# Differential attention: where the ratio of the two softmaxes' sums is formed

## Chip, cores and metric

The kernel runs on 1 core of one Trainium2 chip. The metric is the device time of one execution in microseconds; less is better. It was measured as 2989.36 us, median of 3 runs (2987.06 to 2989.91).

## The reference

The program is two transformer blocks over 1024 tokens of width 1024, float32. The change touches one stage of the second block, differential attention, 4 heads with queries and keys of 64 and values of 128:

```python
s1 = einsum(q1, k1) * scale
s2 = einsum(q2, k2) * scale
p = softmax(s1) - lam * softmax(s2)
out = einsum(p, v)
```

`lam` is one scalar. With e1, e2 the exponentials and t1, t2 their row sums, the kernel uses p = (e1 - lam * t1/t2 * e2) / t1: it forms the ratio t1/t2 times -lam, combines the two unnormalised rows with it, and multiplies the result of the values by 1/t1 at the end.

## The kernel before

The five engines each run a program of stages in order, and semaphores order them against each other. Class `DiffAttention` is the stage in question. It handles M = 32 tiles m of 128 queries (4 heads, 8 tiles each); a tile's scores against all 1024 keys fill two PSUM banks for each of the two softmaxes, c = 0 and c = 1 (banks 0 to 3). In an iteration m of the engines' loops, with no bank spare for the scores:

- **TensorE** (`tensor`): turns the combined weights of tile m-2 in eight transposes (`turn`, L1583, banks 4 and 5), multiplies half of a pair's weights with the values in twelve matmuls (`attend`, L1596), then forms the scores of tile m+1: four matmuls of 512 columns for c = 0 and four for c = 1 (`scores`, L1573). Each of the two groups waits until ScalarE's exponential of tile m has read its banks. Every other iteration it turns two results back (`back`, L1607).
- **ScalarE** (`scalar`): in even iterations it takes a result out (`take`, L1662); it copies the high parts of the turned weights of tile m-2 out of PSUM (`high`, two of 512 columns, L1656); in `exps` it shifts the peak to a bias of one element a partition (L1631) and takes the exponential of c = 0 (L1643, out to tile `both`, with an accumulator read that gives the row sum), then that of c = 1 (L1643 too, out to tile `diff`); in odd iterations it scales two results (`finish`, L1672).
- **VectorE** (`vector`): two peaks of tile m (`peak`, L1696), two low parts of tile m-2 (`low`, L1718), then for tile m-1 `weigh`: the reciprocal of both sums (L1703) and the ratio (L1707, one element a partition), and the `combine` (L1713) over 1024 columns.
- **GpSimd** parts the next head's queries, keys and values into high and low (L1497 to L1532), stores a head's result, and near the end parts the first operands of the next attention (L1225, L1227). SyncE loads them.

So VectorE's order in an iteration is peak, peak, low, low, reciprocal, ratio, combine, and ScalarE's is (take), high, high, bias, exponential, exponential, (finish). The combine of tile m-1 follows the ratio, and TensorE's turn of it follows the combine, one iteration later. A peak of tile m waits for its score group, and the exponential c = 0 for the bias, the exponential c = 1 for the second peak.

Of the kernel before, what the change touches and what calls it, by code (L numbers as in the profile page):

```python
# [25 lines left out]
ACT = mybir.ActivationFunctionType  # L26
ALU = mybir.AluOpType
# [14 lines left out]
class Core:  # L42


    def __init__(self, nc, ctx, words, parts_words):

        self.nc, self.ctx = nc, ctx
        self.parts_words = parts_words
        self.arena = ctx.enter_context(nc.sbuf_tensor("arena", [P, words], F32))
        self.arena_at = nc.sbuf_base - 4 * words  # L50
        self.psum = ctx.enter_context(nc.psum_tensor("psum", [P, 8, HALF], F32))
        self.words, self.top = words, 0
        self.plain, self.parts_ctx = False, None
        self.open_parts("parts_mixer")
        self.free, self.used, self.total_cleared, self.arrivals = [], [], 0, 0
        self.pool_stored = [ctx.enter_context(nc.semaphore(f"pool_stored{s}")) for s in range(2)]
        self.pool_stored_count = [0, 0]
# [69 lines left out]
class Stage:  # L127
# [8 lines left out]
    def scalar(self, act):  # L136
        pass

    def vector(self, dve):
        pass  # L140
# [5 lines left out]
class Part(Stage):  # L146


    def __init__(self, done=(), sync=None, tensor=None, scalar=None, vector=None, gpsimd=None):
        self.done, self.methods = list(done), (sync, tensor, scalar, vector, gpsimd)  # L150
# [47 lines left out]
def hold(engine, conditions):  # L198

    for sem, value in conditions:  # L200
        engine.wait_ge(sem, value)
# [871 lines left out]
class WideAttention:  # L1073
# [286 lines left out]
    def turned_half(self, h):  # L1360
        return self.core.psum[:, 4 + h, :].rearrange("p (b t) -> p b t", t=P)
# [68 lines left out]
class DiffAttention:  # L1430
# [5 lines left out]
    def __init__(self, core, name, q, k, v, out, neg_lam, neg_shift, loads_after, first_free, rest_free, pe_after, act_after, own, sets, shared):  # L1436


        self.core, self.q, self.k, self.v, self.out = core, q, k, v, out
        self.neg_lam, self.neg_shift = neg_lam, neg_shift  # L1440
        self.loads_after, self.first_free, self.rest_free = loads_after, first_free, rest_free
        self.pe_after, self.act_after, self.ahead = pe_after, act_after, []
        self.M = self.HEADS * TT
        self.pT, self.p0 = shared
        here = [own.take(3, S, dtype=F32R) for c in range(2)]
        self.qk = [[sets[0], here[1]], [here[0], sets[1]]]
        self.vp = [sets[2], own.take(2, TT, P, dtype=F32R)]
        self.p1 = own.take(2, S)
        self.qs, self.ks, self.vs = own.take(2, S), own.take(2, S), own.take(TT, self.DV)
        self.os_, self.oT = own.take(2, TT, self.DV), own.take(2 * P)  # L1450
        self.nmax, self.bias, self.ratio = own.take(4), own.take(2), own.take(2)
        self.total, self.inv = own.take(8, 2), own.take(8, 2)
        s = core.sem
        self.loaded, self.v_loaded = core.sems(f"{name}_loaded", 2), s(f"{name}_v_loaded")
        self.parted, self.v_parted = core.sems(f"{name}_parted", 2), s(f"{name}_v_parted")
        self.scored, self.peaked, self.neg_ready, self.shifted, self.expd = (
            s(f"{name}_{x}") for x in ("scored", "peaked", "neg_ready", "shifted", "expd"))
        self.inverted, self.ratio_ready, self.combined = s(f"{name}_inverted"), s(f"{name}_ratio_ready"), core.sems(f"{name}_combined", 2)
        self.opened = s(f"{name}_opened")
        self.turned, self.high_out, self.low_out = s(f"{name}_turned"), s(f"{name}_high_out"), s(f"{name}_low_out")  # L1460
        self.attended, self.taken, self.backed, self.finished = (
            s(f"{name}_{x}") for x in ("attended", "taken", "backed", "finished"))
        self.stored, self.stored_before = core.pool_stored, list(core.pool_stored_count)
        for c in range(2):
            core.pool_stored_count[c] += 16 * self.HEADS // 2
        self.stage_free = core.sems(f"{name}_stage_free", 2)
        self.done = [(self.stage_free[c], self.HEADS // 2) for c in range(2)]
        self.exps_done = [(self.expd, 2 * self.M)]
        self.results_out = [(self.finished, self.M // 2)]
        self.even_set_free = [(self.scored, 6 * TT), (self.attended, 3 * TT // 2)]  # L1470
# [156 lines left out]
    def exps(self, act, m, c):  # L1627
# [14 lines left out]
        src = self.core.psum[:, 2 * c:2 * c + 2, :].rearrange("p a b -> p (a b)")  # L1642
        act.activation(dst, src, ACT.Exp, bias=bias, accum_out=self.total[:, m % 8, c:c + 1]).then_inc(self.expd, 1)  # L1643

    def turned_half(self, h):
        return self.core.psum[:, 4 + h, :].rearrange("p (b t) -> p b t", t=P)

# [27 lines left out]
    def scalar(self, act):  # L1675
        M = self.M
        hold(act, self.act_after)
        for m in range(M + self.LAG):
            if m % 2 == 0 and 0 <= m - 6 < M:
                self.take(act, (m - 6) // 2)  # L1680
            if 0 <= m - 2 < M:
                self.high(act, m - 2)
            if m < M:
                self.exps(act, m, 0)
                self.exps(act, m, 1)
            if m % 2 and 0 <= m - 7 < M:
                self.finish(act, (m - 7) // 2)
# [7 lines left out]
        spot = self.nmax[:, at:at + 1]  # L1695
        dve.tensor_reduce(spot, src, AX.X, ALU.max, negate=True).then_inc(self.neg_ready if c else self.peaked, 1)  # L1696

    def weigh(self, dve, m):

        dve.wait_ge(self.expd, 2 * m + 2)  # L1700
        if m >= 8:
            dve.wait_ge(self.finished, m // 2 - 3)
        dve.reciprocal(self.inv[:, m % 8], self.total[:, m % 8]).then_inc(self.inverted, 1)  # L1703
        dve.wait_ge(self.inverted, m + 1)
        if m >= 2:
            self.wait_combined(dve, m - 2)
        dve.tensor_scalar(self.ratio[:, m % 2:m % 2 + 1], self.total[:, m % 8, 0:1], self.inv[:, m % 8, 1:2], self.neg_lam,  # L1707
                          ALU.mult, ALU.mult).then_inc(self.ratio_ready, 1)

    def combine(self, engine, m):  # L1710

# [9 lines left out]
    def vector(self, dve):  # L1721
        M = self.M
        hold(dve, self.act_after)
        for m in range(M + self.LAG):
            if m < M:
                self.peak(dve, m, 0)
                self.peak(dve, m, 1)
            for h in range(2):
                if 0 <= m - 2 < M:
                    self.low(dve, m - 2, h)  # L1730
            if 0 <= m - 1 < M:
                self.weigh(dve, m - 1)
                if (m - 1) % TT not in self.BY_POOL:
                    self.combine(dve, m - 1)

# [3185 lines left out]
```

## Time and profile before

| | us |
|---|---|
| median of 3 runs | 2989.36 |
| the profiled execution's own time | 2981.91 |
| its span | 2980.2 |
| PE busy | 2830.7 (95%) |
| DVE busy | 1765.6 (59%) |
| POOL busy | 1345.3 (45%) |
| ACT busy | 1174.8 (39%) |
| the stage touched, first to last scores | 2448.1 to 2622.4 |

PE is TensorE's matmuls and PEld its weight loads, DVE VectorE, ACT ScalarE, POOL GpSimd. The shares are over the whole program; the stage touched is about 190 us of it, between the projections of the second layer and the latent attention. PEclk is the granted TensorE clock as a share of full speed. A row of a timeline gives start, duration, engine, line, operation, what it writes and reads, shapes and the number of instructions merged; brackets hold the idle time before and what ended it. Since engines overlap the end of one instruction with the start of the next, the cost of an instruction in a row of them is best read from start to start.

### The profile page before, as it was taken

The numbers are of one execution on the slowest core, as the hardware profiler recorded it, in microseconds if no ns is written. First come the engines' busy times: TensorE is split into PE (matmuls) and PEld (weight loads), VectorE is DVE, ScalarE is ACT, GpSimd is POOL, SyncE is SP. The second block draws the span as 40 slices with busy tenths as digits, with TensorE's granted clock in tenths as the row PEclk, the third lists the DMA queues.
The fourth block names the chain that finished last, engine by engine and source line by source line (L and its number), as shares of the span: only waits on it lengthen the run. The fifth ranks groups of instructions, "written<-read, shape, count | busy, mean of one in ns | idle before, by whom it ended". The sixth has DMA issues, their size and how long they took to land.

```text
span 2980.2 us, 42866 instructions
## 1 busy us (share of the span) xinstructions
PE 2830.7 (95%) x15248; PEld 2379.3 (80%) x15248; DVE 1765.6 (59%) x3125; ACT 1174.8 (39%) x2142; POOL 1345.3 (45%) x962
## 2 busy tenths in 40 slices
PE   7999998899999999999999999999999978889999
PEld 6688957777888878888888788987888776678877
DVE  3799937448666651313057578971224849978861
ACT  3311167243222221313123457761323536767750
POOL 2233124555777776663255334335341534333235
PEclk9999998899999999999999999999999999999999
DMA  3123243332222125443865442405426753131223
GB/s 138 65 96 134 68 115 75 125 113 81 85 85 85 45 88 203 125 141 123 150 203 181 127 113 67 117 22 174 151 84 227 223 152 75 46 79 36 84 85 128
DMA packets 224371, 336.30 MB, mean 113 GB/s; under 512 B 81911, under 2 KB 152439, under 8 KB 223687
## 3 DMA queue, kind: packets, MB, share of 16 engines
q1 hardware_dynamic: 200790, 289.88, 32.4%
q10 hardware_dynamic: 22192, 39.98, 3.7%
q0 software_dynamic: 1216, 4.20, 0.5%
q8 instruction: 102, 1.67, 0.2%
q14 instruction: 71, 0.57, 0.1%
HBM read 235.20 MB, written 98.81 MB: 112 GB/s over the span
## 4 chain that ended last, share of the span: by engine, by line
PE 85%; DVE 5%; issue 3%; ACT 2%; DMA 2%; POOL 1%; SPq 1%; DVEq 0%; POOLq 0%; ACTq 0%; PEldq 0%
PE psum L737 16%; PE psum L2924 15%; PE psum L2568 8%; PE psum L3259 8%; PE psum L444 7%; PE psum L1275 4%; PE psum L1306 4%; PE psum L1286 4%; PE psum L530 3%; PE psum L1573 2%; PE psum L984 2%; PE psum L962 1%; PE psum L973 1%; PE psum L2033 1%; PE psum L2243 1%
## 5 line engine op out<-in xcount | busy, mean ns | idle before, releaser
L2924 PE MATMUL psum<-parts_ffn 128*128 128x512 f32 x1200 | 285.5, 393 | 3.7 <-issue 2.0
L737 PE MATMUL psum<-parts_even,parts_ffn 128*128 128x512 f32 (+1 forms) x1344 | 288.1, 376 | 0.0
L737 PE MATMUL psum<-parts_odd 128*128 128x496 f32 (+1 forms) x1344 | 269.9, 361 | 6.2 <-POOL parts_odd L652 5.3
L737 PEld LDWEIGHTS psum<-parts_even,parts_ffn 128*128 128x128 f32 x1344 | 239.1, 189 | 44.6
L2924 PEld LDWEIGHTS psum<-parts_ffn 128*128 128x128 f32 x1200 | 227.0, 189 | 53.6 <-issue 2.2
L737 PEld LDWEIGHTS psum<-parts_odd 128*128 128x128 f32 x1344 | 227.2, 191 | 41.9 <-POOL parts_odd L652 5.5
L444 PE MATMUL psum<-parts_mixer 128*128 128x512 f32 x912 | 210.0, 391 | 0.3 <-DVE parts_mixer L287 0.3
L444 PEld LDWEIGHTS psum<-parts_mixer 128*128 128x128 f32 x912 | 170.4, 188 | 35.8 <-DVE parts_mixer L287 0.5
L2311 DVE TENSOR_SCALAR_CACHE_REDUCE choose_flags<-arena,choose_bits 128x384 uint8<-128x384 f32 (+2 forms) x198 | 174.3, 943 | 1.2
L3259 PE MATMUL psum<-parts_ffn 128*128 128x512 f32 x720 | 167.3, 389 | 2.9 <-DVE arena L3065 1.6
L2924 PE MATMUL psum<-up_t,parts_ffn 128*128 128x512 f32 x684 | 168.7, 394 | 0.0
L3259 PEld LDWEIGHTS psum<-parts_ffn 128*128 128x128 f32 x720 | 135.0, 188 | 31.9 <-DVE arena L3065 2.1
L773 ACT ACTIVATE arena<-psum 128x512 f32<-128x512 f32 (+4 forms) x120 | 60.6, 520 | 240.7 <-PE psum L737 238.8
L2924 PEld LDWEIGHTS psum<-up_t,parts_ffn 128*128 128x128 f32 x684 | 128.0, 187 | 30.8
L3847 DVE SCALAR_TENSOR_TENSOR arena<-arena 128x64 f32<-128x64 f32 (+1 forms) x464 | 133.9, 369 | 0.6
L402 POOL CAST parts_mixer<-arena 128x1024 fp32r<-128x1024 f32 (+1 forms) x23 | 29.0, 1261 | 225.8 <-PE psum L444 109.1
L2999 ACT ACTIVATE arena<-psum,arena 128x1024 f32<-128x1024 f32 x44 | 53.0, 1207 | 189.9 <-DVE psum L3094 158.9
L3065 DVE SCALAR_TENSOR_TENSOR arena<-psum,arena 128x1023 f32<-128x1023 f32 x88 | 111.0, 1280 | 26.0 <-ACT arena L2999 24.4
L3236 POOL TENSOR_TENSOR parts_ffn<-arena,parts_ffn 128x1024 fp32r<-128x1024 f32 x44 | 118.4, 2691 | 3.5
L2558 POOL TENSOR_TENSOR out_ring<-arena,out_ring 128x1024 fp32r<-128x1024 f32 x48 | 115.7, 2411 | 3.8
L2556 POOL CAST out_ring<-arena 128x1024 fp32r<-128x1024 f32 x48 | 51.6, 1075 | 137.3 <-PE psum L2568 118.8
L1275 PE MATMUL psum<-latent 96*128 96x512 f32 x384 | 101.8, 401 | 1.6 <-ACT both L1341 1.2
(419 smaller groups left out, 6466.4 us busy)
## 6 DMA issues: line engine op xcount, KB each, us to landing
arena<-ffn_down_k SPq DMA_DIRECT2D x44, 512.0 KB, 3.7
arena<-x SPq DMA_DIRECT2D x8, 2048.0 KB, 9.6
x<-arena SPq DMA_DIRECT2D x24, 512.0 KB, 3.9
arena<-w_in_e SPq DMA_DIRECT2D x24, 512.0 KB, 4.6
e_tokens<-arena ACTq DMA_DIRECT2D x24, 512.0 KB, 3.3
arena<-w_in_o SPq DMA_DIRECT2D x24, 496.0 KB, 6.1
arena<-ffn_up_b SPq DMA_DIRECT2D x11, 1024.0 KB, 4.9
up_raw_two<-ffn_up_b SPq DMA_DIRECT2D x11, 1024.0 KB, 4.9
```

The costliest lines, as they stand in the source:

```text
L444: last = pe.matmul(self.bank(s, h), self.weights.parts[:, s, a, k, :], self.hT[:, b, k, h * HALF:(h + 1) * HALF], start=(k, a, b) == (0, 0 ...
L737: last = pe.matmul(self.bank(t, n), self.hT[:, a, k, t * P:(t + 1) * P], w, start=(k, a, b) == (0, 0, 0), stop=(k, a) == (KT - 1, 1))
L1275: last = pe.matmul(ps[:, 2 * (n % 2) + b, :], queries, keys[:, b * HALF:(b + 1) * HALF], start=m == 0, stop=m == len(pairs) - 1)
L1286: last = pe.transpose(ps[:, 4 + h, j * P:(j + 1) * P], self.p[:, n % 2, b * P:(b + 1) * P], self.core.ident)
L1306: last = pe.matmul(ps[:, 6, 0:2 * P], values, self.pT[:, g % 2, part, b], start=(b, m) == (0, 0), stop=(b, m) == (KT - 1, len(pairs) - 1))
L2311: last = dve.tensor_scalar(self.flags[j], w, self.bits[:, j:j + 1].bitcast(F32), None, op, ALU.add, accum_out=self.count[:, j:j + 1])
L2558: pool.tensor_tensor(low, self.raw[:, n % 2], high.bitcast(F32), ALU.subtract).then_inc(self.w_low, 1)
L2568: last = pe.matmul(self.core.psum[:, 2 * t + h, :], self.catT[:, b, k, (4 * g + t) * P:(4 * g + t + 1) * P], w[:, c, h * HALF:(h + 1) * HA ...
L2924: last = pe.matmul(self.core.psum[:, bank, :], slot[:, a, k, :], operand[b][:, k, :], start=opens and (k, a, b) == (0, 0, 0), stop=(k, a) ...
L3236: pool.tensor_tensor(low, self.raw[:, n % 2], high.bitcast(F32), ALU.subtract).then_inc(self.w_low, 1)
L3259: last = pe.matmul(self.core.psum[:, 2 * t + h, :], a[:, b, t * P:(t + 1) * P], w[:, c, h * HALF:(h + 1) * HALF], start=(k, m) == (0, 0), ...
L3847: last = dve.scalar_tensor_tensor(out=x, in0=x, scalar=self.ss[:, n % 2, head + h:head + h + 1], in1=gain, op0=ALU.mult, op1=ALU.mult)
```

## The change

ScalarE, not VectorE, forms the ratio. In iteration m it does so for tile m-1 between its two exponentials, in two one-element copies: the sum t1 times the reciprocal of t2, and, after a wait for that, the result times -lam. `weigh` on ScalarE waits for VectorE's reciprocal and, for its two-deep buffer, for the combine of tile m-3. VectorE keeps the reciprocal, now in `invert`, and does it ahead of the low parts instead of behind them; the combine stays behind the low parts.

```diff
@@ -1448,13 +1448,14 @@
         self.p1 = own.take(2, S)
         self.qs, self.ks, self.vs = own.take(2, S), own.take(2, S), own.take(TT, self.DV)
         self.os_, self.oT = own.take(2, TT, self.DV), own.take(2 * P)
-        self.nmax, self.bias, self.ratio = own.take(4), own.take(2), own.take(2)
+        self.nmax, self.bias, self.ratio, self.share = own.take(4), own.take(2), own.take(2), own.take(2)
         self.total, self.inv = own.take(8, 2), own.take(8, 2)
         s = core.sem
         self.loaded, self.v_loaded = core.sems(f"{name}_loaded", 2), s(f"{name}_v_loaded")
         self.parted, self.v_parted = core.sems(f"{name}_parted", 2), s(f"{name}_v_parted")
         self.scored, self.peaked, self.neg_ready, self.shifted, self.expd = (
             s(f"{name}_{x}") for x in ("scored", "peaked", "neg_ready", "shifted", "expd"))
+        self.shared = s(f"{name}_shared")
         self.inverted, self.ratio_ready, self.combined = s(f"{name}_inverted"), s(f"{name}_ratio_ready"), core.sems(f"{name}_combined", 2)
         self.opened = s(f"{name}_opened")
         self.turned, self.high_out, self.low_out = s(f"{name}_turned"), s(f"{name}_high_out"), s(f"{name}_low_out")
@@ -1642,6 +1643,16 @@
         src = self.core.psum[:, 2 * c:2 * c + 2, :].rearrange("p a b -> p (a b)")
         act.activation(dst, src, ACT.Exp, bias=bias, accum_out=self.total[:, m % 8, c:c + 1]).then_inc(self.expd, 1)
 
+    def weigh(self, act, m):
+
+        share, ratio = self.share[:, m % 2:m % 2 + 1], self.ratio[:, m % 2:m % 2 + 1]
+        act.wait_ge(self.inverted, m + 1)
+        if m >= 2:
+            self.wait_combined(act, m - 2)
+        act.activation(share, self.total[:, m % 8, 0:1], ACT.Copy, scale=self.inv[:, m % 8, 1:2]).then_inc(self.shared, 1)
+        act.wait_ge(self.shared, m + 1)
+        act.activation(ratio, share, ACT.Copy, scale=self.neg_lam).then_inc(self.ratio_ready, 1)
+
     def turned_half(self, h):
         return self.core.psum[:, 4 + h, :].rearrange("p (b t) -> p b t", t=P)
 
@@ -1682,6 +1693,9 @@
                 self.high(act, m - 2)
             if m < M:
                 self.exps(act, m, 0)
+            if 0 <= m - 1 < M:
+                self.weigh(act, m - 1)
+            if m < M:
                 self.exps(act, m, 1)
             if m % 2 and 0 <= m - 7 < M:
                 self.finish(act, (m - 7) // 2)
@@ -1695,17 +1709,12 @@
         spot = self.nmax[:, at:at + 1]
         dve.tensor_reduce(spot, src, AX.X, ALU.max, negate=True).then_inc(self.neg_ready if c else self.peaked, 1)
 
-    def weigh(self, dve, m):
+    def invert(self, dve, m):
 
         dve.wait_ge(self.expd, 2 * m + 2)
         if m >= 8:
             dve.wait_ge(self.finished, m // 2 - 3)
         dve.reciprocal(self.inv[:, m % 8], self.total[:, m % 8]).then_inc(self.inverted, 1)
-        dve.wait_ge(self.inverted, m + 1)
-        if m >= 2:
-            self.wait_combined(dve, m - 2)
-        dve.tensor_scalar(self.ratio[:, m % 2:m % 2 + 1], self.total[:, m % 8, 0:1], self.inv[:, m % 8, 1:2], self.neg_lam,
-                          ALU.mult, ALU.mult).then_inc(self.ratio_ready, 1)
 
     def combine(self, engine, m):
 
@@ -1725,11 +1734,12 @@
             if m < M:
                 self.peak(dve, m, 0)
                 self.peak(dve, m, 1)
+            if 0 <= m - 1 < M:
+                self.invert(dve, m - 1)
             for h in range(2):
                 if 0 <= m - 2 < M:
                     self.low(dve, m - 2, h)
             if 0 <= m - 1 < M:
-                self.weigh(dve, m - 1)
                 if (m - 1) % TT not in self.BY_POOL:
                     self.combine(dve, m - 1)
 

```

## Rows read from the trace of the kernel before

**Rows 1.** The chain that ended last, 2556 to 2584 us, by line.

```profile
by line: PE psum L1573 42.6%; issue 18.2%; ACT both L1656 11.3%; PE psum L1583 11.1%; PE psum L1596 10.3%; ACT both L1643 4.6%; PE psum L1607 2.3%; ACT diff L1631 2.0%; ACTq L1655 0.3%; ACTq L1669 0.1%; ACTq L1661 0.1%
```

**Rows 2.** Windows: length, then busy us (x instructions) by engine, clock, DMA.

```profile
core 0: us, PE busy (x) PEld busy (x) DVE busy (x) ACT busy (x) POOL busy (x), PEclk, DMA share, GB/s
2506.00:2513.00 7.00, 5.42 (x31) 4.20 (x32) 6.89 (x9) 5.18 (x13) 2.00 (x1) 1.00 0.56 121
2475.00:2626.00 151.00, 130.32 (x802) 106.15 (x801) 147.11 (x194) 107.37 (x230) 42.12 (x23) 1.00 0.20 53
2448.00:2475.00 27.00, 18.92 (x55) 13.29 (x56) 21.76 (x22) 13.72 (x26) 22.52 (x12) 0.69 0.76 178
```

**Rows 3.** Waits, 2475 to 2626 us: total, times, longest.

```profile
PEld psum L1573 <- ACT diff L1643: 8.0, 24, 0.3
...
DVE diff L1696 <- PE psum L1573: 1.3, 7, 0.2
```

**Rows 4.** Timeline of PE: start, us; in brackets idle before.

```profile
2567.28 1.20 PE L1573 MATMUL psum<-diff_even 128*128 128x512 f32 x4 [0.73 <-ACT both L1643]
2568.38 1.19 PE L1573 MATMUL psum<-diff 128*128 128x512 f32 x4
2569.40 0.38 PE L1607 MATMUL psum<-arena,diff 128*128 128x128 f32 x2
2569.62 1.03 PE L1583 MATMUL psum<-arena,both 128*128 128x128 f32 x8
...
2572.81 1.20 PE L1573 MATMUL psum<-diff_even 128*128 128x512 f32 x4 [0.73 <-ACT both L1643]
...
2578.14 1.19 PE L1573 MATMUL psum<-diff_even 128*128 128x512 f32 x4 [0.72 <-ACT both L1643]
```

**Rows 5.** Timeline of ACT.

```profile
2562.89 0.62 ACT L1672 ACTIVATE diff<-psum,diff 128x128 f32<-128x128 f32 x2
2563.39 0.40 ACT L1662 ACTIVATE diff<-psum 128x256 f32<-128x256 f32 x1
...
2570.26 1.08 ACT L1656 ACTIVATE both<-psum 128x512 fp32r<-128x512 f32 x2 [1.93 <-PE psum L1583]
2571.23 0.29 ACT L1631 ACTIVATE diff<-diff,arena 128x1 f32<-128x1 f32 x1
2571.55 1.11 ACT L1643 ACTIVATE both<-psum,diff 128x1024 f32<-128x1024 f32 x1
2572.57 0.19 ACT L1643 ACTIVATION_READ_ACCUMULATOR both<-psum,diff 128x1 f32 x1
2572.66 1.11 ACT L1643 ACTIVATE diff<-psum,diff 128x1024 f32<-128x1024 f32 x1
```

**Rows 6.** Timeline of DVE.

```profile
2568.53 2.35 DVE L1696 TENSOR_REDUCE diff<-psum 128x1 f32<-128x1024 f32 x2
2570.89 1.29 DVE L1718 TENSOR_TENSOR both<-psum,both 128x512 fp32r<-128x512 f32 x2
2572.09 0.15 DVE L1703 RECIPROCAL diff<-diff 128x2 f32<-128x2 f32 x1
2572.28 0.27 DVE L1707 TENSOR_SCALAR diff<-diff,diff,arena 128x1 f32<-128x1 f32 x1
2572.59 1.28 DVE L1713 SCALAR_TENSOR_TENSOR both<-diff,diff,both 128x1024 f32<-128x1024 f32 x1
2574.05 2.36 DVE L1696 TENSOR_REDUCE diff<-psum 128x1 f32<-128x1024 f32 x2 [0.17 <-PE psum L1573]
```

**Rows 7.** Timelines of DVE and PE, a long combine.

```profile
2506.07 3.01 DVE L1713 SCALAR_TENSOR_TENSOR both<-diff,diff,both 128x1024 f32<-128x1024 f32 x1
...
2509.14 1.09 PE L1583 MATMUL psum<-arena,both 128*128 128x128 f32 x8 [0.65 <-DVE both L1713]
```

**Rows 8.** Timeline of PE at the stage's start.

```profile
2465.57 1.71 PE L1573 MATMUL psum<-diff_even 128*128 128x512 f32 x4 [2.15 <-ACT both L1643]
2467.09 1.91 PE L1573 MATMUL psum<-diff 128*128 128x512 f32 x4
```

**Rows 9.** Timelines of POOL and DVE in the drain.

```profile
2630.42 2.34 POOL L1227 TENSOR_TENSOR latent<-latent,latent 96x1024 fp32r<-96x1024 f32 x1
...
2631.32 2.52 DVE L1713 SCALAR_TENSOR_TENSOR both<-diff,diff,both 128x1024 f32<-128x1024 f32 x1
```

## The prediction

> **What bounds the kernel now.** I read four views of the differential attention, the stage the diff touches, and counted times from X, the start of a first exponential (L1643, out to `both`) on ScalarE. The chain of waits comes first [rows 1]: in steady state it runs through TensorE's scores (L1573), the turns (L1583), ScalarE's copies of the high parts (L1656) and its first exponential; VectorE's lines are not in it. The windows [rows 2] seem to say otherwise: from 2475 to 2626 us VectorE is busy 147.11 of 151 us, TensorE 130.32, ScalarE 107.37. So VectorE looks like the bound and ScalarE like the engine with room, and that must be settled by the waits. VectorE waited only 1.3 us for scores, but TensorE's weight loads for the second score group waited 24 times, 0.3 us each, for the second exponential, `diff` L1643 [rows 3].
>
> The timelines give the loop in one step. The first exponential starts at 2571.55 = X [rows 5]. The next first score group starts at 2572.81, X + 1.26, when that exponential has left its banks [rows 4]. The second exponential starts at 2572.66, X + 1.11, and with a like hand-over, 1.25 from its start, it allows the second group at X + 2.36. In the step before, the two groups start at 2567.28 and 2568.38, 1.10 apart, and 1.26 + 1.10 is 2.36 as well. **The two score groups and the two exponentials are level to within 0.1 us.** Then: second group 1.03 (2568.38 to 2569.40, where the turns back or the turns begin), the turns' first half until ScalarE's high parts 0.64 (2569.62 to 2570.26), high parts 0.97 (to 2571.23), bias 0.32 (to 2571.55). Sum 1.11 + 1.25 + 1.03 + 0.64 + 0.97 + 0.32 = 5.32, which is the short step (2572.81 to 2578.14, 5.33). The long step adds two transposes back before the turns, 2569.40 to 2569.62, and is 5.53. Mean 5.43.
>
> VectorE's own work in a step, start to start: two peaks 2.36 (2568.53 to 2570.89), low parts 1.20, reciprocal 0.19, ratio 0.31, and the combine, 1.28 long: 5.34 at most. After it VectorE waited 0.17 for scores [rows 6]. It is close behind the loop's 5.43, not in it.
>
> **The change, part by part.** There are 32 steps.
>
> (a) VectorE's tensor_scalar (L1707) goes: start to start 2572.28 to 2572.59, 0.31 a step, 9.9 us of VectorE's time in all [rows 6]. It lies beside the loop, so I credit **0**. The most that it could give, were VectorE the pacing engine in the 27 steps at full clock, is 27 x 0.31 = 8.4 us.
>
> (b) The reciprocal moves ahead of the low parts. The low parts come 0.19 us later; the next turns into their banks come most of a step later, so **0**. Its wait for the exponentials is long met at its new place, with or without the low parts ahead of it.
>
> (c) ScalarE gets two one-element copies with a pointer scale, the second waiting for the first, between the first and second exponentials. No row shows this operation. Nearest from above is the bias (L1631, one element, pointer operand): 0.29 long, and 2571.23 to 2571.55 = 0.32 to an operation that waits for it [rows 5]. That is the price of the first copy. The second exponential does not wait for the ratio, so it may start inside the second copy. The two 128-element copies with pointer scale at 2562.89 take 0.62 together and the next operation starts 0.50 after them: 0.25 a piece though each is 0.37 long, 0.12 overlapped. For 0.29 that leaves 0.17 to 0.18. I take **0.32 + 0.18 = 0.50**. The low bound is 0.32 + 0.10 = 0.42, 0.10 being the step from the accumulator read to the next exponential (2572.57 to 2572.66); the high bound is 2 x 0.33 = 0.66, with no overlap.
>
> Behind this pair on ScalarE stand the second exponential, the finish, the take and the high parts. ScalarE has room before the high parts, but **the second exponential has none**: it releases the second score group, which is already waited for. So the second group starts at X + 1.11 + 0.50 + 1.25 = X + 2.86 instead of 2.36, and turns, high parts, bias and the next first exponential follow 0.50 later. TensorE gets a new gap of 0.5 between its two groups. Delays in score pairs 5 to 31 count at full clock: 27 x 0.50 = **+13.5 us** (bounds 27 x 0.42 = 11.3 and 27 x 0.66 = 17.8).
>
> (d) At the start, pairs 2 to 4 run at 0.69 of the clock on average [rows 2], and there the groups start 1.52 apart, 2465.57 and 2467.09 [rows 8], 0.42 more than at full clock. Of 0.50 0.08 is left, or a little more where the first peaks are waited for: 3 x 0.17 = **+0.5** (bounds 0 and 1).
>
> (e) VectorE's combine now waits for a ratio that ScalarE begins at X + 1.43 and ends at about X + 1.72. It started at X + 1.04 (2572.59), so it comes 0.7 later and ends at X + 3.0. The peaks queue behind it; they start at X + 3.0, where the first group is done at about X + 2.5. The turns need the combine, and TensorE reaches them at X + 2.86 + 1.03 = X + 3.9: 0.9 spare. The bias needs the peak at X + 5.6 and has it by X + 4.2. **0**. VectorE will now idle about 1 us a step before the combine. Were the ratio over 0.9 us later than reckoned, that would be the next thing on the loop.
>
> (f) Combine and GpSimd's two-input operations exclude each other in the trace: the combine at 2506.07 took 3.01 in place of 1.28, and the turns waited for it, 0.65 [rows 7]. The spare time before the turns stays 0.9, so such meetings cost what they did; which ones happen changes with the phase: **0**, bounds -0.8 and +0.8. In the drain the last combine met one: 2631.32, 2.52 long, behind a GpSimd subtraction from 2630.42 to 2632.76 [rows 9]. In the drain, too, the combine before it is 0.7 later, while reciprocal and ratio no longer stand between low parts and the last combine (2572.09 to 2572.59, 0.50): +0.2. The last combine then falls some 1 us later against GpSimd and may miss that meeting, worth 1.24. I take half: **-0.6** (bounds -1.24 and 0).
>
> Sum: 13.5 + 0.5 + 0.2 - 0.6 = **+13.6 us**. Lowest 11.3 + 0 + 0.2 - 1.2 - 0.8 = 9.5; highest 17.8 + 1 + 0.2 + 0 + 0.8 = 19.8. The stages behind hang on this stage's end and shift by the same. The profiled execution took 2981.91 us (span 2980.2), 7.5 below the median of 2989.36; so it would become 2995.5 and the median 3003.0.
>
> **A rule that speaks for the change.** VectorE's row shows 0.31 start to start for one element, nearly all of it not arithmetic [rows 6]. The Trainium skill, "VectorE: DVE Perf Modes", Rules for kernel authors, says of chained VectorE operations to minimize the operation count, as each drains in any case. Removing one per step is what the change does; by that rule alone the time would fall by up to 8.4 us. The rows say that this engine isn't the one that ends the step.
>
> **Rivals.** *VectorE paces (faster).* For: busy 97% of the full-clock stretch, and its own work a step is within 0.1 us of 5.43. The place is the peaks behind the combine: if scores wait for nothing but banks that VectorE frees, the step shortens by up to 0.31, 27 x 0.31 = 8.4 us, to 2981. It decides only if the copies' 0.50 on ScalarE is hidden, so if the second exponential has over 0.5 us of room. Against: the 24 waits of 0.3 us [rows 3]. Chance 0.07.
>
> *The delay is absorbed (no change).* ScalarE waits 1.93 before its high parts in a long step. If the second score group did not need the second exponential so promptly, both changes would lie beside the loop: 2989.4, 0.05.
>
> *TensorE's clock falls (much slower).* The granted clock was 1.00 from 2475 to 2626 us, with TensorE busy 86%, and 0.69 from 2448 to 2475 with 70% [rows 2]. After the change it is busy in about 4.7 of 5.93 us, 79%, with two gaps a step instead of one. For 1.00: from 2506 to 2513 the clock stayed there at 5.42 of 7 us, 77%, with a gap of 0.65 beside the 0.7 of every step [rows 7]. Against: that was one step, not thirty. A loop at 1.2 GHz costs at least the second group and the turns' first half over again, 0.6 + 0.3, about +1.0; if half of the 27 loops ran so, +13.5 more, 3016, and with all of them more than 3030. The Trainium skill, "TensorE: Matmul & The Clock Gate", A second HAM failure mode, describes a kernel whose short idles between groups of matmuls kept the clock switching between its levels. Chance 0.08.
>
> **How the numbers follow.** My forecast has 0.80. Its bounds of 9.5 and 19.8 give 2998.9 and 3009.2; the three runs spread 1.5 us either way, so 2998 to 3011. That leaves out the three rivals, 0.20 together. About 0.2% (6 us) can be told from no change. Slower 0.80 + 0.08 = 0.88, same 0.05, faster 0.07.
>
> **What would show it.** In the profile after: on ScalarE, the second exponential 1.6 after the first, with two operations of 0.26 to 0.30 between; TensorE idle 0.4 to 0.6 between its score groups, released by the second exponential; steps of 5.83 and 6.04 in turn; VectorE's busy share down from 97% to about 84%, idle before the combine with ScalarE as releaser; granted clock still 1.00 in the middle. I am wrong if the steps stay at 5.32 and 5.53, if the copies take over 0.33 a piece (or load a table), or if the clock falls.

## The result and the profile after

The changed kernel took 3002.72 us, median of 11 runs, against 2989.36 us; the ratio is 1.004 (95% interval 1.003 to 1.005). It is slower by 13.4 us; 13.6 were forecast.

The profiled execution took 3003.22 us, 21.3 more than the one shown of before. I cut both spans at the stage touched, from its first scores to the first scores of the latent attention behind it:

| us | before | after | difference |
|---|---|---|---|
| start to first scores | 2448.1 | 2455.5 | +7.4 |
| scores of tile 0 to those of tile 5 | 31.0 | 32.0 | +1.0 |
| scores of tile 5 to those of tile 31 | 142.6 | 156.6 | +14.0 |
| scores of tile 31 to the latent scores | 21.3 | 20.2 | -1.1 |
| latent scores to the end of the span | 337.3 | 337.3 | 0.0 |

So the stage itself is longer by 14.0 us, 194.8 to 208.8. The 7.4 us ahead of it are in work that the change doesn't touch, and are looked at under what was not expected. The first five steps run partly at the lower clock; the 26 steps from tile 5 to tile 31 are the loop proper, and I call what comes behind them the drain.

The page's head, the span and the busy times:

```profile
span 3001.5 us, 42898 instructions
...
PE 2844.2 (95%) x15248; PEld 2391.2 (80%) x15248; DVE 1756.6 (59%) x3093; ACT 1189.4 (40%) x2206; POOL 1342.3 (45%) x962
```

VectorE is 9.0 us less busy than before, ScalarE 14.6 more: the work did move as meant. What it did to the waits, from 2487 to 2645 us:

```profile
DVE both L1722 <- ACT diff L1654: 25.4, 27, 1.1
...
PE psum L1574 <- ACT diff L1644: 10.6, 26, 0.4
```

VectorE's combine (now L1722) waits for ScalarE's ratio in 27 steps, 25.4 us. TensorE itself, not only its weight loads as in [rows 3], now waits 26 times, 0.4 us each, for the second exponential. TensorE's timeline is to be held against [rows 4]:

```profile
2572.71 1.20 PE L1574 MATMUL psum<-diff_even 128*128 128x512 f32 x4 [0.73 <-ACT both L1644]
...
2578.76 1.20 PE L1574 MATMUL psum<-diff_even 128*128 128x512 f32 x4 [0.72 <-ACT both L1644]
2580.36 1.21 PE L1574 MATMUL psum<-diff 128*128 128x512 f32 x4 [0.41 <-ACT diff L1644]
2581.41 1.04 PE L1584 MATMUL psum<-arena,both 128*128 128x128 f32 x8
...
2584.60 1.21 PE L1574 MATMUL psum<-diff_even 128*128 128x512 f32 x4 [0.73 <-ACT both L1644]
```

The two groups start 1.60 apart where it was 1.10, with a gap of 0.41 that ends on the second exponential, and the steps are 6.05 (2572.71 to 2578.76) and 5.84 (2578.76 to 2584.60), for 5.53 and 5.33. ScalarE's timeline shows what stands in between, against [rows 5]:

```profile
2577.51 1.11 ACT L1644 ACTIVATE both<-psum,diff 128x1024 f32<-128x1024 f32 x1
...
2578.61 0.28 ACT L1652 ACTIVATE diff<-diff,diff 128x1 f32<-128x1 f32 x1
2578.93 0.29 ACT L1654 ACTIVATE diff<-diff,arena 128x1 f32<-128x1 f32 x1
2579.13 1.10 ACT L1644 ACTIVATE diff<-psum,diff 128x1024 f32<-128x1024 f32 x1
```

The first copy costs 0.32 to the start of the second, and the second exponential starts 0.20 into the second copy. From first to second exponential it is 1.62 in place of 1.11. VectorE's timeline, against [rows 6]:

```profile
2579.26 1.28 DVE L1722 SCALAR_TENSOR_TENSOR both<-diff,diff,both 128x1024 f32<-128x1024 f32 x1 [1.13 <-ACT diff L1654]
```

The combine starts at 2579.26, which is 1.75 after the first exponential at 2577.51 (the prediction's X), after 1.13 us of idleness; it ends at 2580.54, 0.87 before TensorE begins the turns at 2581.41. In such a step VectorE waits for ScalarE, and TensorE doesn't wait for VectorE. And the window with the clock:

```profile
2487.00:2640.00 153.00, 121.96 (x729) 96.82 (x730) 128.74 (x152) 112.15 (x267) 41.43 (x22) 1.00 0.14 39
```

TensorE is busy 80% of the time, where it was 86%, and is still granted full speed throughout.

### The profile page after: what moved, and what is told of

Read it like the earlier page. It is cut to its first block, busy times and chain, and to the rows that moved or that the text cites. A ratio compares the mean times of both kernels' runs of the same rounds, so it can differ in the third digit from the quotient of the medians.

```text
span 3001.5 us, 42898 instructions
## 1 busy us (share of the span) xinstructions
PE 2844.2 (95%) x15248; PEld 2391.2 (80%) x15248; DVE 1756.6 (59%) x3093; ACT 1189.4 (40%) x2206; POOL 1342.3 (45%) x962
## 3 DMA queue, kind: packets, MB, share of 16 engines
q8 instruction: 102, 1.67, 0.2%
## 4 chain that ended last, share of the span: by engine, by line
PE 83%; DVE 5%; ACT 4%; issue 3%; DMA 2%; SPq 1%; POOL 1%; PEld 0%; DVEq 0%; POOLq 0%; ACTq 0%; PEldq 0%
PE psum L737 16%; PE psum L2934 14%; PE psum L2578 8%; PE psum L3269 8%; PE psum L444 7%; PE psum L1275 4%; PE psum L1306 4%; PE psum L1286 4%; PE psum L530 3%; PE psum L984 2%; PE psum L1574 1%; PE psum L962 1%; PE psum L973 1%; ACT both L1667 1%; PE psum L2253 1%
```

## The experiments

Every kernel ran beside runs of the kernel before on the same chip, and its ratio is to those, whose median was 2988.6 or 2989.0 us. The stage is measured as above, in the one profiled execution of each. I call it a meeting when VectorE's combine falls on one of GpSimd's subtractions and takes up to 3.5 us in place of 1.28. "Clean" steps are those without a meeting and without a change of head. The stage's length holds the meetings and the low clock at its start and end too, so a difference of one to four microseconds between two kernels says little by itself; the clean steps say more.

| kernel | stage, us | clean steps, us | median, us | ratio to before (95%) |
|---|---|---|---|---|
| before | 194.8 | 5.33 / 5.53 | 2989.4 | |
| after | 208.8 | 5.84 / 6.05 | 3002.7 | 1.004 (1.003 to 1.005) |
| the reciprocal alone | 198.6 | 5.33 / 5.54 | 2990.6 | 1.0007 (0.9993 to 1.0021) |
| the copies alone | 206.7 | 5.83 / 6.05 | 3000.3 | 1.0034 (1.0022 to 1.0047) |
| a third copy | 216.6 | 6.16 / 6.38 | 3008.8 | 1.0055 (1.0040 to 1.0070) |
| copies behind the exponentials | 227.2 | 6.17 / 6.18 | 3019.6 | 1.0104 (1.0089 to 1.0119) |
| copies in ScalarE's wait | 194.6 | 5.33 / 5.54 | 2988.5 | 1.0002 (0.9990 to 1.0013) |
| before, bias early | 191.5 | 5.12 / 5.21 | 2986.1 | 0.9989 (0.9979 to 1.0000) |
| after, bias early | 201.5 | 5.51 / 5.72 | 2997.4 | 1.0026 (1.0014 to 1.0039) |
| copies in the wait, bias early | 188.4 | 5.00 / 5.21 | 2983.0 | 0.9977 (0.9967 to 0.9987) |

**The copies alone.** Is the second exponential's delay the whole cost, or does the late combine have a part? The kernel before keeps its ratio on VectorE, and ScalarE makes the same two copies to a place that nobody reads. The reciprocal stands ahead of the low parts, as in the change (not shown in the cut; what that is worth alone is measured below).

```diff
                 self.exps(act, m, 0)
+            if 0 <= m - 1 < M:
+                self.copies(act, m - 1)
+            if m < M:
                 self.exps(act, m, 1)
```

> The kernel before with the two copies on ScalarE between its exponentials, their result unused; VectorE still forms the ratio itself, the reciprocal ahead of the low parts. Theory (the delay of the second exponential is the whole cost, the late combine costs nothing): steps of 5.84 and 6.05, first scores to latent scores 207 to 210 us, median 3001 to 3004. Rival (the combine that waits for ScalarE's ratio carries part of the cost): under 205 us. Rival (VectorE paces): 195 us.

VectorE's and TensorE's timelines of one step:

```profile
2582.48 1.28 DVE L1728 SCALAR_TENSOR_TENSOR both<-diff,diff,both 128x1024 f32<-128x1024 f32 x1
...
2582.77 1.20 PE L1574 MATMUL psum<-diff_even 128*128 128x512 f32 x4 [0.72 <-ACT both L1644]
2584.38 1.20 PE L1574 MATMUL psum<-diff 128*128 128x512 f32 x4 [0.41 <-ACT diff L1644]
...
2588.82 1.20 PE L1574 MATMUL psum<-diff_even 128*128 128x512 f32 x4 [0.72 <-ACT both L1644]
```

VectorE has its ratio in time and starts the combine at 2582.48, ahead of TensorE's scores, not after a wait for ScalarE. Still the score groups start 1.61 apart and the step is 6.05. So in a clean step the lateness of the combine costs nothing; the clean steps of the two kernels agree to 0.01.

The stage is 206.7, 2.1 less than with the change and just under the 207 to 210 expected, the median 3000.3 just under 3001. Of the 2.1 us, 1.5 lie in two steps, 6.75 and 6.82 us with the change, 6.05 and 6.03 here. The step of 6.82, in VectorE's and TensorE's timelines of the changed kernel:

```profile
2553.97 3.13 DVE L1722 SCALAR_TENSOR_TENSOR both<-diff,diff,both 128x1024 f32<-128x1024 f32 x1 [1.12 <-ACT diff L1654]
...
2557.16 1.09 PE L1584 MATMUL psum<-arena,both 128*128 128x128 f32 x8 [0.83 <-DVE both L1722]
```

The same step with the copies alone:

```profile
2552.04 3.24 DVE L1728 SCALAR_TENSOR_TENSOR both<-diff,diff,both 128x1024 f32<-128x1024 f32 x1
...
2555.34 1.09 PE L1584 MATMUL psum<-arena,both 128*128 128x128 f32 x8
```

Both combines met GpSimd. But this one started 0.83 after its first exponential (2551.21) and the late one 1.74 after (2552.23), so that here TensorE had hardly to wait. In this step, then, lateness did cost: with the copies alone the meeting adds 0.2, with the change 1.0. In the other step, 6.75, the changed kernel had a meeting and this one had none; that is a matter of where the meetings fall.

**A third copy.** One more copy that waits for the ratio, its result unused, makes the suspected cost larger and leaves the rest.

```diff
         act.activation(ratio, share, ACT.Copy, scale=self.neg_lam).then_inc(self.ratio_ready, 1)
+        act.wait_ge(self.ratio_ready, m + 1)
+        act.activation(spare, ratio, ACT.Copy, scale=self.neg_lam)
```

> The change with a third one-element copy on ScalarE behind the ratio, waiting for it, result unused. Theory: each step is longer by one more dependent copy, 0.32 us: steps of 6.16 and 6.37, first scores to latent scores 208.8 + 30 x 0.32 = 218 us, median about 3012. Rival (part of the 0.5 us lay in room that is now used up, or the cost is the wait for the reciprocal): less than 213 us.

ScalarE's timeline:

```profile
2580.28 1.11 ACT L1644 ACTIVATE both<-psum,diff 128x1024 f32<-128x1024 f32 x1
...
2581.39 0.28 ACT L1652 ACTIVATE diff<-diff,diff 128x1 f32<-128x1 f32 x1
2581.70 0.30 ACT L1654 ACTIVATE diff<-diff,arena 128x1 f32<-128x1 f32 x1
2582.03 0.29 ACT L1657 ACTIVATE diff<-diff,arena 128x1 f32<-128x1 f32 x1
2582.23 1.09 ACT L1644 ACTIVATE diff<-psum,diff 128x1024 f32<-128x1024 f32 x1
```

Starts 0.31, 0.33 and 0.20 apart; the second exponential comes 1.95 after the first, and the steps grew from 5.84 and 6.05 to 6.16 and 6.38. The stage grew by 7.8 us, less than the 9 forecast, as its longest meetings made steps of 6.50 and 6.42 where the change has 6.82 and 6.75; the median of 3008.8 is below the 3012 forecast too. In the clean steps the whole 0.33 of the third copy shows.

**Copies behind the exponentials.** This gives the second exponential its old place back and makes the ratio later still.

```diff
-            if 0 <= m - 1 < M:
-                self.weigh(act, m - 1)
             if m < M:
                 self.exps(act, m, 1)
+            if 0 <= m - 1 < M:
+                self.weigh(act, m - 1)
```

> The change with ScalarE's two copies moved behind the second exponential instead of between the two. Theory (what costs is what the place delays): the second exponential and the second score group go back to 1.1 us after the first ones, but the ratio is ready only at about X + 2.8, the combine ends at X + 4.1, and TensorE, which reaches the turns at X + 3.4 or X + 3.6, waits for it 0.75 or 0.55 us. Steps of 6.1 in place of 5.84 and 6.05; from the first scores to the first of the latent attention about 213 us (208.8 with the change, 194.8 before), median about 3007. Rival A (the copies cost their 0.5 us wherever they stand on ScalarE): 209 us, 3003. Rival B (only the delay of the second exponential costs): 195 us, 2989.

The clean steps came as the theory had them. VectorE's and TensorE's rows of one, with the turns released by the combine:

```profile
2583.64 1.28 DVE L1722 SCALAR_TENSOR_TENSOR both<-diff,diff,both 128x1024 f32<-128x1024 f32 x1 [1.37 <-ACT diff L1654]
...
2584.99 1.09 PE L1584 MATMUL psum<-arena,both 128*128 128x128 f32 x8 [0.42 <-DVE both L1722]
```

They also decide against both rivals: a fixed price on ScalarE asked for 5.84 and 6.05, the exponential's delay alone for 5.33 and 5.53, and the steps are 6.17 and 6.18. But the stage is 227.2, far over the 213 forecast. That forecast had carried the mean step and forgotten what its own mechanism implies: with no time to spare between combine and turns, every meeting is paid in full. Six of the later steps took 7.1 to 9.1 us. One of them, in the timelines of VectorE, TensorE and GpSimd, and the windows of 4 us on both sides of it:

```profile
2514.42 3.10 DVE L1722 SCALAR_TENSOR_TENSOR both<-diff,diff,both 128x1024 f32<-128x1024 f32 x1 [1.37 <-ACT diff L1654]
...
2517.58 1.09 PE L1584 MATMUL psum<-arena,both 128*128 128x128 f32 x8 [2.23 <-DVE both L1722]
2518.43 2.60 PE L1597 MATMUL psum<-both,diff_even 128*128 128x256 f32 x12
...
2514.08 2.36 POOL L1507 TENSOR_TENSOR diff<-diff,diff 128x1024 fp32r<-128x1024 f32 x1
...
2514.00:2518.00 4.00, 1.77 (x11) 1.30 (x11) 3.58 (x2) 0.36 (x2) 2.37 (x2) 1.00 0.21 26
2518.00:2522.00 4.00, 4.00 (x22) 3.72 (x20) 3.05 (x5) 3.69 (x8) 0.00 (x0) 0.60 0.95 223
```

The combine takes 3.10 for 1.28, 1.82 more, and this step is 8.00 us, 1.83 over the clean 6.17. TensorE stands still 2.23 us, and then its granted clock is 0.60 in the next window; inside it, from 2519 to 2522, it is 0.50, the lower level of 1.2 GHz. The values' twelve matmuls took 2.60 in place of 1.67. That cost this step nothing, as the next scores, at 2520.83, come 1.26 after their exponential's start at 2519.57, as in the clean steps.

**The reciprocal alone.**

```diff
                 self.peak(dve, m, 1)
+            if 0 <= m - 1 < M:
+                self.invert(dve, m - 1)
             for h in range(2):
```

> The kernel before with one part of the change alone: VectorE's reciprocal ahead of the low parts, the ratio still on VectorE. Theory: no cost and no gain, steps of 5.3 and 5.5, 194 to 196 us from first scores to latent scores, median 2989. Rival (low parts 0.2 later hold the turns): 27 x 0.2 = 5 us more.

The ratio's interval holds 1, and the middle part, tile 5 to tile 31, is 142.5 us for 142.6. The stage missed its forecast, 198.6 for 194 to 196: 1.1 us at the start and 2.8 in the drain, where the last combine met GpSimd and took 3.15 us, and TensorE's values behind it took 2.91 and 2.90 in place of 1.67. The median can't tell such an amount: the interval reaches to 1.0021, 6 us. Moving the reciprocal costs nothing in the loop.

**Copies in ScalarE's wait.** Here VectorE loses its operation as in the change, but the second exponential isn't delayed.

```diff
+            if 0 <= m - 1 < M:
+                self.weigh(act, m - 1)
             if 0 <= m - 2 < M:
                 self.high(act, m - 2)
             if m < M:
                 self.exps(act, m, 0)
-            if 0 <= m - 1 < M:
-                self.weigh(act, m - 1)
-            if m < M:
                 self.exps(act, m, 1)
...
+            if 0 <= m - 1 < M:
+                self.invert(dve, m - 1)
             if m < M:
                 self.peak(dve, m, 0)
                 self.peak(dve, m, 1)
-            if 0 <= m - 1 < M:
-                self.invert(dve, m - 1)
```

> The change with both copies moved to where ScalarE waits for the turns, ahead of its high parts, and VectorE's reciprocal moved ahead of the peaks so that it is ready in time. VectorE still has one operation less than before. Theory (the loop does not contain VectorE): steps of 5.3 and 5.5 as before, 194 to 196 us, median 2989. Rival (VectorE paced the kernel before): steps shorter by up to 0.3, 187 us, median 2981. Rival (the copies cost 0.5 wherever they stand): 209 us.

Timelines of ScalarE, VectorE and TensorE:

```profile
2585.21 0.29 ACT L1652 ACTIVATE diff<-diff,diff 128x1 f32<-128x1 f32 x1 [0.23 <-DVE diff L1716]
2585.54 0.29 ACT L1654 ACTIVATE diff<-diff,arena 128x1 f32<-128x1 f32 x1
2586.92 1.09 ACT L1667 ACTIVATE both<-psum 128x512 fp32r<-128x512 f32 x2 [1.09 <-PE psum L1584]
...
2585.01 0.17 DVE L1716 RECIPROCAL diff<-diff 128x2 f32<-128x2 f32 x1 [0.41 <-ACT diff L1644]
...
2583.93 1.20 PE L1574 MATMUL psum<-diff_even 128*128 128x512 f32 x4 [0.73 <-ACT both L1644]
...
2589.57 1.16 PE L1574 MATMUL psum<-diff 128*128 128x512 f32 x4 [0.82 <-ACT both L1644]
```

The same two copies now cost nothing; ScalarE still waits 1.09 us behind them for the turns. The score groups of this pair start 5.64 apart, as they do where a head changes, and the clean steps are as before. And taking an operation from VectorE gained nothing, with 0.31 us a step free: it waits for the exponential ahead of its reciprocal, 0.41 here. ScalarE's work, then, has no price of its own. That VectorE didn't pace the kernel before is shown less strictly here, as the reciprocal's new place gives VectorE a new wait; the next experiment shortens the steps with VectorE's work unchanged, and is free of that.

**Bias early.** If the loop is as the prediction reads it, its last term, the bias of one element between the high parts and the first exponential, should come off it when moved into ScalarE's wait. It was tried on the kernel before, on the changed kernel, and together with the last experiment.

```diff
             if m < M:
+                self.shift(act, m)
             if 0 <= m - 2 < M:
                 self.high(act, m - 2)
             if m < M:
                 self.exps(act, m, 0)
```

`shift` is the bias's wait and activation, taken out of `exps`.

> The kernel before with ScalarE's one-element bias moved ahead of the high parts, into its wait for the turns. Theory: it takes 0.32 us off the loop, which would be 5.11 on average; VectorE's own 5.17 then paces, so steps shorten by 0.26: about 188 us from first scores to latent scores, median about 2982. Rival (the loop as read is wrong, and VectorE paces already): no change, 195 us. Rival (the bias now waits for its peak and holds the high parts): slower than 195.

> The change with the bias moved ahead of the high parts. Theory: steps of 5.52 and 5.73, 208.8 - 27 x 0.32 = 200 us, median about 2994. VectorE has room here, so the whole 0.32 shows. Rival (something else than this loop sets the steps after the change): under 0.2 a step, over 203 us.

> Bias ahead of the high parts, and the ratio's two copies on ScalarE also ahead of them, with VectorE's reciprocal ahead of the peaks. Theory: the loop is 5.0 and 5.2, VectorE's own work 4.9, so here the operation taken off VectorE should pay: 186 us from first scores to latent scores, median about 2980, 1 to 2 us better than the bias alone. Rival (ScalarE's wait is too short for three operations and the high parts slip): 188 us or more.

On the changed kernel the whole 0.33 a step shows (5.84 to 5.51). On the kernel before only 0.21 of it shows in the short steps, which stay at 5.12, and all 0.32 in the long ones. The totals came out dearer than forecast, 191.5 us for 188 (median 2986.1 for 2982) and 201.5 for 200 (2997.4 for 2994), with two meetings in each that made steps of 6.91 and 6.92, and of 7.44 and 6.59. VectorE's timeline in the kernel before with the bias early:

```profile
2580.80 2.35 DVE L1700 TENSOR_REDUCE diff<-psum 128x1 f32<-128x1024 f32 x2
...
2584.76 1.28 DVE L1717 SCALAR_TENSOR_TENSOR both<-diff,diff,both 128x1024 f32<-128x1024 f32 x1
2585.96 2.35 DVE L1700 TENSOR_REDUCE diff<-psum 128x1 f32<-128x1024 f32 x2
```

From these peaks to the next it is 5.16, with no idle time in between, and the mean of 5.12 and 5.21 is 5.165. The loop alone would give 5.01 and 5.21, 5.11 on average. Here VectorE does set the short steps, and here the operation taken off it pays: with the ratio on ScalarE too they are 5.00. ScalarE's timeline of that last kernel, with ratio and bias both in its wait:

```profile
2585.32 0.34 ACT L1654 ACTIVATE diff<-diff,diff 128x1 f32<-128x1 f32 x1
2585.69 0.29 ACT L1656 ACTIVATE diff<-diff,arena 128x1 f32<-128x1 f32 x1
2586.18 0.29 ACT L1631 ACTIVATE diff<-diff,arena 128x1 f32<-128x1 f32 x1 [0.20 <-DVE diff L1713]
2586.46 1.09 ACT L1669 ACTIVATE both<-psum 128x512 fp32r<-128x512 f32 x2
2587.43 1.12 ACT L1646 ACTIVATE both<-psum,diff 128x1024 f32<-128x1024 f32 x1
```

Both copies, the bias (which waits 0.20 for its peak), the high parts and the first exponential follow each other closely; ScalarE's wait for the turns is gone. The rival's number for a slipping of the high parts, 188 or more, was met, but not its mechanism: the steps are the 5.0 and 5.2 of the theory. This version beats both kernels: 2983.0 us, ratio 0.9977 (0.9967 to 0.9987). Its stage of 188.4 missed the 186 forecast through two steps of 6.91 and 6.79 us, meetings again. That it beats the early bias on the old kernel is shown by the clean steps (5.00 against 5.12). The stages, 188.4 and 191.5, differ by more than that gives: 2.0 of the 3.1 us lie ahead of tile 5. The two medians, 2983.0 and 2986.1, point the same way, but their intervals overlap.

## Why the prediction was right

**The loop and its place (the heart of it).** Right. Score groups and exponentials were level, so the second exponential had no room. The copies alone, unused, lengthen the step by the same 0.5; out of that place they cost nothing.

**The price (c).** 0.50 was taken, 0.51 to 0.52 measured: 0.32 to the second copy as on the bias row, and 0.20 to the exponential for the 0.18 reckoned. The copies last 0.28 and 0.29.

**The VectorE operation (a) and the reciprocal (b).** Credited at 0, and 0 by the experiments with the reciprocal alone and with the copies in ScalarE's wait. On the rule cited from the Trainium skill, "VectorE: DVE Perf Modes", Rules for kernel authors: the operation did weigh 0.31 on VectorE, but with VectorE off the loop the runs show no gain from having one fewer. It paid only after the bias had been moved, and then 0.12 in the short steps. VectorE's own work was reckoned at 5.34 a step, at most. Where it has no wait at all, with the bias early, it takes 5.16, since the peaks start 1.20 after the combine and not 1.28; it was further from pacing than the prediction's "within 0.1 us" has it.

**The start (d).** +0.5 forecast, +1.0 measured, but not by the prediction's mechanism. Of it 0.9 lies in one step, 4.07 to 4.96, and that is TensorE's clock in the scores of tile 1, the group for the first softmax. TensorE's rows of that group before, after, and with the reciprocal alone:

```profile
2454.50 1.19 PE L1573 MATMUL psum<-diff_even 128*128 128x512 f32 x4 [2.61 <-ACT both L1643]
```

```profile
2461.86 2.08 PE L1574 MATMUL psum<-diff_even 128*128 128x512 f32 x4 [2.64 <-ACT both L1644]
```

```profile
2452.49 2.08 PE L1573 MATMUL psum<-diff_even 128*128 128x512 f32 x4 [2.64 <-ACT both L1643]
```

The same four matmuls took 1.19 at full speed in the execution shown of before and 2.08 after; so they did in seven of the other eight kernels, the reciprocal alone and the early bias among them, and at this point nothing that was changed has run yet. The 0.9 belongs to these executions, not to the change. The next three steps, in which copies run, grew by 0.08, 0.05 and 0.01, where 3 x 0.17 had been forecast: by these two executions nearly all of the 0.50 is hidden there.

**The combine (e).** It was to start 0.7 later than X + 1.04; it starts at X + 1.75, with 0.87 us spare before the turns for the 0.9 reckoned.

**Meetings with GpSimd (f).** Forecast at 0; between tiles 5 and 31 they cost 2.1 us where it had been 1.4, inside the bounds of 0.8 either way. The reason given doesn't hold, though: the spare time before the turns did not stay at 0.9. By the prediction's own times it was 1.1 before (the combine ends at X + 2.32, the turns are reached at X + 3.39), and the long combine of [rows 7] says the same: 1.73 longer, 0.65 of it waited for. It is 0.87 now. The late combine has taken 0.2 us of protection from each meeting.

In the drain the last combine missed its meeting, as thought possible. VectorE's and GpSimd's rows, against [rows 9]:

```profile
2655.20 1.28 DVE L1722 SCALAR_TENSOR_TENSOR both<-diff,diff,both 128x1024 f32<-128x1024 f32 x1
...
2652.97 2.37 POOL L1227 TENSOR_TENSOR latent<-latent,latent 96x1024 fp32r<-96x1024 f32 x1
```

The combine took 1.28, not 2.52, as GpSimd's subtraction ends at 2655.34, when the combine has barely begun. I had taken half of those 1.24 us; all came. The prediction also left out TensorE's clock behind it. The last turns before and after:

```profile
2633.90 1.97 PE L1583 MATMUL psum<-arena,both 128*128 128x128 f32 x8 [2.85 <-DVE both L1713]
```

```profile
2656.53 1.09 PE L1584 MATMUL psum<-arena,both 128*128 128x128 f32 x8 [0.39 <-DVE both L1722]
```

Before, TensorE ran them and part of the values at the lower clock, behind a gap of 2.85 us (granted 0.66 from 2633 to 2638 us). In the changed kernel the low clock fell on the turns ahead of these (0.72 from 2650 to 2656 us), and from 2656 to 2664 us it was 1.00. From the last turns to the latent scores it is 7.70 us in place of 9.00, and up to them 12.45 from the scores of tile 31 in place of 12.26.

**The rivals.** VectorE paces: out. The delay is absorbed: out. The clock falls: it stayed at full speed from 2487 to 2640 us at 80% busy. The Trainium skill, "TensorE: Matmul & The Clock Gate", A second HAM failure mode, tells of short idles that kept the clock switching; two gaps of 0.4 and 0.7 us a step didn't do that here. With the copies behind the exponentials a gap of 2.23 us was followed by a fall to 0.60, but one of 2.40 eight microseconds earlier was not.

**The sum.** The loop and the price of the copies are right by their mechanism: 26 steps of 0.51 to 0.52 are 13.4 of the 14.0 us, and that term carries the forecast. That 13.6 and 14.0 agree so well is partly luck. The loop gave 0.4 more than reckoned for these steps, the start 0.5 more and the meetings 0.7 more, and the drain, with the last pair's 0.5 in it, 1.2 less (-1.1 for +0.1). The medians differ by 13.4, and their interval is 9 to 15 us.

## What to carry to other kernels

A busy share of 97% on one engine and 71% on another does not say where work can be put. What says it is which wait ends last, and then the place within the engine's order: the same two copies cost 0.5 us a step between two exponentials, about 1.0 behind both, meetings included, and nothing in a wait a few instructions on. A result that comes later, but still in time, is free only in a step in which nothing else is late. Before moving work off a busy engine, find the loop and shorten that; the relief pays only once the busy engine has become part of it.

## What was not expected

**The stages ahead move by nearly as much as the effect.** The first scores of this stage start between 2446.1 and 2456.6 us in the ten profiled executions, though nothing ahead of it was changed. It arises between 427 us, where the kernels before and after are still level to 0.3 us, and 582 us, in the first block: there the chain's long stretch of matmuls starts at 582.3 us before and at 590.8 after, 581.6 with the reciprocal alone and 590.8 with the copies alone. Windows from 440 to 560 us, before and then after:

```profile
440.00:560.00 120.00, 100.61 (x681) 93.16 (x680) 82.64 (x167) 73.69 (x163) 61.85 (x32) 0.85 0.30 75
```

```profile
440.00:560.00 120.00, 102.77 (x621) 93.81 (x621) 84.75 (x164) 70.30 (x156) 49.70 (x25) 0.77 0.25 59
```

The granted clock averaged 0.85 in one and 0.77 in the other; it was 0.75 with the copies alone, whose stage started at 2455.5, and 0.84 with the reciprocal alone, whose stage started at 2446.1. That the clock is the cause and not a consequence of other waits there was not tested. It isn't the change: were the 7.4 us its own, the medians would differ by 21 and not by 13.4. It may be behind the spread of the changed kernel's single executions, 2992 to 3007 us, and it is why the stage's steps decide here where single totals can't.

**How dear a meeting with GpSimd is depends on the spare time behind the combine.** In the steps compared the combine stretches to 3.1 or 3.2 us. With about 1.8 us spare, as with the copies alone, that cost 0.2; with the change's 0.9 it costs 1.0 (6.82 for 5.80, the clean step behind a change of head); with none it is paid in full. The dearest, 9.06 for 6.26, had a combine of 3.25 and then turns at the lower clock, 1.97 for 1.09.
